# Query-key products of eight attention maps: three passes over 64 rows, or two passes of 128 and 64 rows

## The chip, the cores and the metric

The kernel runs on one core of a Trainium2 chip. The metric is the device time of one execution in microseconds, lower is better. The core has a matrix engine (TensorE, PE in the profile, with its weight loads as PEld), three engines for elementwise work (VectorE is DVE, ScalarE is ACT, GpSimd is POOL) and SyncE (SP), which issues most of the transfers. Each engine works through its own instructions in order and waits on semaphores.

## The reference, cut to what matters

The reference computes two transformer blocks over a sequence of 512 positions with model width 1024, in float32. The change lies in the second block's attention, which has 16 query-key products of head dimension 64:

```python
# stick-breaking attention, 8 heads (S in the kernel)
z = einsum('bhqd,bhkd->bhqk', q, k) * scale          # d = 64, S = 512
...
# differential attention, 4 heads of 2 maps (D in the kernel)
logits = einsum('bhqd,bhkd->bhqk', q, k) * scale + bias
probs = softmax(where(causal, logits, -inf))
w = probs[:, :, 0] - lam * probs[:, :, 1]
out = einsum('bhqk,bhkd->bhqd', w, v)
```

Both are causal, so of the 4 x 4 blocks of 128 x 128 only the lower triangle is computed: four matmuls of 128, 256, 384 and 512 columns for a map.

## The kernel before, in words

Every matrix product is made from float32 values that are split in a high part (rounded to the matrix engine's fp32r format) and a low part, the rest. A product is three matmuls ("passes") into the same accumulator: high x high, high x low and low x high. The helper `mm3` (L1723) issues them, through `mm` (L1720), so that nearly all matmuls have line L1721.

The order of the work is a plan, a list of small steps that `make_plan` (L121) writes out by hand. Each engine walks through the same list and does its own part of each step; semaphore waits are counted from the plan. Weights come in 312 units of 128 x 1024 values. SyncE loads unit u+3 when unit u has been split (L773 to L776); ACT makes the high part `wh`, DVE the low part `wl`.

In the attention stage (units 204 to 227) the plan mixes two kinds of matrix work. One is the projection: "single" steps, each three passes of 128 rows x 512 columns with a weight tile, and "vg" steps with 256 columns. The other is the heads. The pieces of the heads stand in the table `ATT_AT` (L60): a key `(224, 5)` says behind which eighth of which unit they come, and `D5.0` is step 0 of the differential pair n=5.

After the two units of a pair n are done, the step `aqev` (L1014 for ACT, L1442 for DVE) writes four tiles into a slot of `aq`: high and low of the query part (index 0 and 1) and high and low of the key part (2 and 3), each [128, 512]. Rows 0 to 63 belong to one head or map and rows 64 to 127 to the other. `aq` has three slots, used in turn. The query-key products read 64 rows of it:

- S steps 0 (L2030 to L2043) compute head b of an even n, keys stationary, columns 384, 128, 256, 512 in this order, each with `mm3`: 12 matmuls.
- D steps 0 and 3 (L2080 to L2093) compute map m = 0 or 1 of an odd n, queries stationary, columns 512, 128, 256, 384: 12 matmuls.
- The heads of n=0 are computed together by step S2 (L2006).

```python
for i in (3, 0, 1, 2):
    w = 128 * (i + 1)
    t = mm3(ps[:, ROFF[i]:ROFF[i] + w], q[pp, 0, 128 * i:128 * i + 128],
            q[pp, 1, 128 * i:128 * i + 128], q[pp, 2, 0:w], q[pp, 3, 0:w], True, True)
```

`pp` is rows 0 to 63 or 64 to 127. The order of pairs in the plan is n = 0, 1, 2, 3, 4, 5, 7, 6. D5.0, the first map of pair 5, comes behind (224, 5); the last `aqev` of pair 5 comes behind (223, 7), with the short steps `S41.0` in between in the plan of unit 223.

During the attention stage the residual x is saved to memory by POOL (step `upx`, L1677, semaphore `s_spill`), and the memory of x takes the attention outputs, one 512-column slice after another. Slices 2, 3, 5, 6 and 7 are written only by later heads. `R1`, `ssq` and `ssg` are not read in the later part of the stage.

Of the kernel before, what the change touches and what calls it, by code (L numbers as in the profile page):

```python
# [7 lines left out]
F32 = mybir.dt.float32  # L8
F32R = mybir.dt.float32r
# [373 lines left out]
def _build(nc, D, out, ctx):  # L383
    plan = make_plan()

    def sem(name):
        return ctx.enter_context(nc.semaphore(name))

    def sb(name, shape, dt=F32, stack=None):
        return (stack or ctx).enter_context(nc.sbuf_tensor(name, shape, dt))  # L390
# [9 lines left out]
    eps5 = sb("eps5", [128, 1])  # L400
    rcs = sb("rcs", [128, 4, 4])
    sb("pad", [128, 88])
    x = sb("x", [128, 8, 512])
    xh = sb("xh", [128, 8, 512], F32R)
    xl = sb("xl", [128, 8, 512], F32R)
    wraw = sb("wraw", [128, 3, 1024])
    wh = sb("wh", [128, 3, 1024], F32R)
    wl = sb("wl", [128, 3, 1024], F32R)
    R = sb("R", [128, 512])
    R1 = sb("R1", [128, 512])  # L410
    ssq = sb("ssq", [128, 512])
    ssg = sb("ssg", [128, 512])
    ones = sb("ones", [128, 128])
    onesr = sb("onesr", [128, 128], F32R)
    ident = sb("ident", [128, 128])
# [163 lines left out]

    def sig(name, **emits):
        return Sig(sem(name), plan, **emits)

# [23 lines left out]
    s_tb = sem("s_tb")  # L608
    s_misc, s_bif, s_spill, s_mg, s_p = (sem(n) for n in ("s_misc", "s_bif", "s_spill", "s_mg", "s_p"))
    s_mgb = [sem(f"s_mgb{j}") for j in range(8)]  # L610
    s_back = [sem(f"s_back{i}") for i in range(2)]
    s_b8 = [sem(f"s_b8{i}") for i in range(2)]
    s_out = [sem(f"s_out{j}") for j in range(8)]
# [146 lines left out]
    @block.sync  # L760
    def _(e):
        def load(u):
            e.dma_start(wraw[:, u % 3, :], units[u]).then_inc(s_w[u % 3], 16)

        for kind, *a in plan:
            if kind == "init":
                for j in range(8):
                    e.dma_start(x[:, j, :], D["xT"][:, j, :]).then_inc(s_x[j], 16)
                    if j == 1:
                        part(e, 3)  # L770
                    if j == 3:
                        load(2)
            elif (kind == "split" or (kind == "split0" and a[0] >= 2)) and \  # L773
                    (u := a[0] if kind == "split" else a[0] - 2) + 3 < NU:
                e.wait_ge(*wl_done(u))
                load(u + 3)  # L776
            elif kind == "last":
                for n, j in enumerate(END_ORDER):
                    if n % 2:
                        e.wait_ge(*(end_g if j in (2, 5) else end_d).at("x", j))  # L780
                        e.dma_start(out[:, j, :], x[:, j, :]).then_inc(s_out[j], 16)
                for j in END_ORDER:
                    e.wait_ge(s_out[j], 16)
# [935 lines left out]
    def _(e):  # L1719
# [3 lines left out]
        def mm3(dst, ah, al, bh, bl, start, stop, skip=False):  # L1723
            mm(dst, ah, bh, start, False, skip)
            mm(dst, ah, bl, False, False, skip)
            return mm(dst, al, bh, False, stop, skip)
# [19 lines left out]
        for kind, *a in plan:  # L1746
# [276 lines left out]
            elif kind == "S":  # L2023
# [6 lines left out]
                if s == 0:  # L2030
                    e.wait_ge(*aq_d.at(n, 1))
                    if head_before["S", n, b]:
                        e.wait_ge(*head_free(head_before["S", n, b]))
                    elif c == 1:
                        e.wait_ge(*av_d.at(0, 0, 3))
                    else:
                        e.wait_ge(*nm_a.at("R1"))
                    for i in (1, 3, 2, 0):
                        t = mm3(ps[:, OFF[i]:OFF[i] + 512 - 128 * i], q[pp, 2, 128 * i:128 * i + 128],
                                q[pp, 3, 128 * i:128 * i + 128], q[pp, 0, 128 * i:512], q[pp, 1, 128 * i:512],  # L2040
                                i != 3, True, skip=True)
                        if i in (2, 0):
                            t.then_inc(S_p.sem, 1)  # L2043
                elif s == 5:
                    if (n, b) == (6, 0):
                        unread(bank(2), 8)
                    for half, group in enumerate(((1, 3, 2), (0,))):
                        e.wait_ge(*S_d.at(n, b, f"l{half}"))
                        if (n, b, half) == (0, 1, 0):
                            e.wait_ge(*att_g.at("tri"))  # L2050
                        for i in group:
                            dst = ps[:, OFF[i]:OFF[i] + 512 - 128 * i]
                            r = slice(OFF[i], OFF[i] + 512 - 128 * i)
                            mm(dst, tri[:, :], hh[:, r], False, False, True)
                            t = mm(dst, tri[:, :], ll[:, r], False, i == 3, True)
                            for j in range(i + 1, 4):
                                w = slice(OFF[j], OFF[j] + 512 - 128 * j)
                                dj = dst[:, 128 * (j - i):]
                                mm(dj, onesn[:, :], hh[:, w], False, False, True)
                                t = mm(dj, onesn[:, :], ll[:, w], False, j == 3, True)  # L2060
                        t.then_inc(S_p.sem, 1)
                elif s == 9:
                    o = ps[:, 0:512]
                    if (n, b) == (6, 0):
                        unread(bank(2), 7)
                    for j in (1, 2, 3, 0):
                        e.wait_ge(*S_d.at(n, b, "x1" if j == 0 else "x0"))
                        e.wait_ge(*av_d.at(0, n // 4, j))
                        r = slice(OFF[j], OFF[j] + 512 - 128 * j)
                        w = slice(64 * (n - n % 2), 64 * (n - n % 2) + 128)  # L2070
                        t = mm3(o[:, 128 * j:512], av[:, j, 0, w], avl[:, j, 0, w], hh[:, r], ll[:, r], j == 1, j == 0,
                                skip=True)
                    t.then_inc(S_p.sem, 1)
            elif kind == "D":
# [5 lines left out]
                if s in (0, 3):  # L2080
                    m = 0 if s == 0 else 1
                    pp = slice(64 * m, 64 * m + 64)
                    if m == 0:
                        e.wait_ge(*aq_d.at(n, 1))
                        e.wait_ge(*head_free(head_before["D", n]))
                    else:
                        e.wait_ge(*D_d.at(n, "r02"))
                    for i in (3, 0, 1, 2):
                        w = 128 * (i + 1)
                        t = mm3(ps[:, ROFF[i]:ROFF[i] + w], q[pp, 0, 128 * i:128 * i + 128],  # L2090
                                q[pp, 1, 128 * i:128 * i + 128], q[pp, 2, 0:w], q[pp, 3, 0:w], True, True)
                        if i in (3, 2):
                            t.then_inc(D_p.sem, 1)  # L2093
                elif s == 7:
                    if n == 7:
                        e.wait_ge(*D_d.at(n, "r12"))
                    for j in range(4):
                        for i in range(3, j - 1, -1):
                            if n == 7 and j == 0 and i >= 2:
                                unread(bank(1), 7)  # L2100
                            if j == 0 and i >= 2:
                                e.wait_ge(*D_d.at(n, "w3" if i == 3 else "w2"))
                            t = e.transpose(ps[:, OFF[j] + 128 * (i - j):OFF[j] + 128 * (i - j) + 128],  # L2103
                                            pm0[:, ROFF[i] + 128 * j:ROFF[i] + 128 * j + 128], ident[:, :])
                        if j in (0, 3):
                            t.then_inc(D_p.sem, 1)
                elif s == 10:
                    o = ps[:, 0:512]
                    w = slice(128 * h, 128 * h + 128)
                    for j in range(4):  # L2110
                        if j < 2:
                            e.wait_ge(*D_d.at(n, f"l{j}"))
                        e.wait_ge(*av_d.at(1, h // 2, j))
                        r = slice(OFF[j], OFF[j] + 512 - 128 * j)
                        t = mm3(o[:, 128 * j:512], av[:, j, 1, w], avl[:, j, 1, w], hh[:, r], ll[:, r], j == 0, j == 3)
                    t.then_inc(D_p.sem, 1)
                elif s == 12:
                    if n == 7:
                        unread(bank(1), 4)
                    e.wait_ge(*D_a.at(n, "sq"))  # L2120
                    col_sums(ps[:, 512:1024], pm0).then_inc(D_p.sem, 1)
                elif s == 15:
                    e.wait_ge(*D_d.at(n, "dg"))
                    mm(ps[:, 512:1024], ones[:, :], pm0[:, 0:512]).then_inc(D_p.sem, 1)
# [171 lines left out]
```

## Time and profile before

| what | value |
|---|---|
| median of 3 runs | 1918.7 us (1918.05 to 1920.92) |
| the profiled execution's own time | 1917.96 us |
| its span, first to last instruction | 1916.1 us |
| mean granted TensorE clock | 0.996 |
| instructions in the span | 21280 |
| PE matmuls | 8718 |

The span is a little shorter than the execution's time, which also holds what lies ahead of the first and behind the last profiled instruction (1.86 us). A row of the timeline gives the start in us, the length in us, the engine, the line, the operation, the tiles as out<-in, the form (rows x stationary columns, rows x moving columns) and how many equal instructions were merged. The length of one matmul includes its way through the array; matmuls overlap, so what one costs in a stream is the distance between its start and the next start.

### The profile page before, as it was taken

Reading aid. Unit: us, or ns where it says so; the run is one execution under the profiler, and the core shown is the slowest. Engines: PE = TensorE matmul, PEld = TensorE weight load, DVE = VectorE, ACT = ScalarE, POOL = GpSimd, SP = SyncE. Lnnn points to the kernel's source line nnn. Section 1 sums busy time; section 2 is a strip of 40 time slices with the busy share of each in tenths; the row PEclk is TensorE's granted clock in tenths of the full one; section 3 lists DMA queues with packets and bytes.
Section 4 is the critical chain, followed back from the end, with each engine's and each line's share of the span. In section 5 each row is a group of like instructions: output and inputs, shape, how many; then the busy total and the mean of one; then the engine's idle time right before and its main releaser. Section 6 shows DMA issues by size and latency. Waiting matters only on the chain.

```text
span 1916.1 us, 21280 instructions
## 1 busy us (share of the span) xinstructions
PE 1892.6 (99%) x8718; PEld 1559.7 (81%) x8718; DVE 1019.6 (53%) x1283; ACT 794.5 (41%) x1060; POOL 227.7 (12%) x257
## 2 busy tenths in 40 slices
PE   9999999999999999999999999999999999999997
PEld 7888888878888788888888888888878888888885
DVE  4444443347354666664344444655565777774335
ACT  5423222236444566442232222555564444443234
POOL 2000001201300111130000022100004100000212
PEclk9999999999999999999999999999999999999998
DMA  4432322342241322423323223322113323233231
GB/s 159 157 108 88 99 99 98 103 149 93 77 138 61 98 88 87 144 88 99 99 89 109 91 96 100 121 67 67 67 44 110 100 88 109 89 98 104 96 110 55
DMA packets 51937, 188.98 MB, mean 99 GB/s; under 512 B 6568, under 2 KB 6824, under 8 KB 50944
## 3 DMA queue, kind: packets, MB, share of 16 engines
q1 hardware_dynamic: 46512, 166.09, 26.1%
q0 software_dynamic: 4176, 19.82, 3.0%
q8 instruction: 69, 1.13, 0.2%
q10 hardware_dynamic: 1152, 1.71, 0.2%
q14 instruction: 28, 0.23, 0.0%
HBM read 179.18 MB, written 11.03 MB: 99 GB/s over the span
## 4 chain that ended last, share of the span: by engine, by line
PE 95%; DVE 2%; ACT 2%; issue 1%; DMA 0%; DVEq 0%; ACTq 0%
PE psum L1721 95%; ACT at L798 1%; DMA wraw<-in_w_ffn 0%; PE psum L2103 0%; DVE x L1130 0%; ACT wh L798 0%; DVE wl L1136 0%; DVE at L1485 0%; DVE sl L1136 0%; ACT L794 0%; DVE bst L1231 0%; DVE az L1133 0%; ACT tm L798 0%; DVEq L379 0%; DVE al L1136 0%
## 5 line engine op out<-in xcount | busy, mean ns | idle before, releaser
L1721 PE MATMUL psum<-xh,wh 128*128 128x512 f32 x1760 | 694.6, 395 | 3.0 <-DVE xl L1133 2.7
L1721 PE MATMUL psum<-xh,wl 128*128 128x512 f32 x1760 | 685.8, 390 | 0.0
L1721 PE MATMUL psum<-xl,wh 128*128 128x512 f32 x1760 | 685.8, 390 | 0.0
L1136 DVE TENSOR_TENSOR wl<-wraw,wh 128x1024 fp32r<-128x1024 f32 (+1 forms) x314 | 401.1, 1285 | 402.7 <-ACT wh L798 401.7
L798 ACT ACTIVATE wh<-wraw 128x1024 fp32r<-128x1024 f32 (+1 forms) x314 | 325.6, 1047 | 367.6 <-PE psum L1721 363.9
L1721 PEld LDWEIGHTS psum<-xh,wh 128*128 128x128 f32 x1760 | 330.8, 188 | 80.5 <-issue 12.0
L1721 PEld LDWEIGHTS psum<-xl,wh 128*128 128x128 f32 x1760 | 330.9, 188 | 69.8 <-issue 2.9
L1721 PEld LDWEIGHTS psum<-xh,wl 128*128 128x128 f32 x1760 | 330.8, 188 | 69.3
L1583 POOL TENSOR_TENSOR ssq<-x 128x512 f32<-128x512 f32 x5 | 5.2, 1040 | 714.4 <-DVE x L1215 454.1
L1721 PE MATMUL psum<-wh,xh 128*128 128x512 f32 (+1 forms) x256 | 88.3, 345 | 0.4 <-ACT zv L798 0.4
L1721 PE MATMUL psum<-wh,xl 128*128 128x512 f32 (+1 forms) x256 | 86.0, 336 | 0.0
L1721 PE MATMUL psum<-wl,xh 128*128 128x512 f32 (+1 forms) x256 | 86.0, 336 | 0.0
L1721 PE MATMUL psum<-hha,wh 128*128 128x512 f32 x176 | 68.5, 389 | 0.0
L1721 PE MATMUL psum<-hla,wh 128*128 128x512 f32 x176 | 68.5, 389 | 0.0
L1721 PE MATMUL psum<-hha,wl 128*128 128x512 f32 x176 | 68.5, 389 | 0.0
L1721 PE MATMUL psum<-hhb,wh 128*128 128x512 f32 x176 | 68.5, 389 | 0.0
L1721 PE MATMUL psum<-hlb,wh 128*128 128x512 f32 x176 | 68.5, 389 | 0.0
L1721 PE MATMUL psum<-hhb,wl 128*128 128x512 f32 x176 | 68.5, 389 | 0.0
L1721 PE MATMUL psum<-hhc,wh 128*128 128x512 f32 x176 | 68.5, 389 | 0.0
L1721 PE MATMUL psum<-hlc,wh 128*128 128x512 f32 x176 | 68.5, 389 | 0.0
L1721 PE MATMUL psum<-hhc,wl 128*128 128x512 f32 x176 | 68.5, 389 | 0.0
L1133 DVE SCALAR_TENSOR_TENSOR ftc<-ftc,cols 128x511 f32<-128x511 f32 x88 | 64.1, 749 | 7.9 <-ACT ftc L798 6.4
(303 smaller groups left out, 2210.1 us busy)
## 6 DMA issues: line engine op xcount, KB each, us to landing
wraw<-in_w_ffn SPq DMA_DIRECT2D x86, 512.0 KB, 3.2
wraw<-in_w_down SPq DMA_DIRECT2D x44, 512.0 KB, 3.2
wraw<-in_w_up SPq DMA_DIRECT2D x44, 512.0 KB, 3.4
wraw<-in_w_qg SPq DMA_DIRECT2D x28, 512.0 KB, 3.3
wraw<-in_w_att SPq DMA_DIRECT2D x24, 512.0 KB, 3.3
wraw<-in_w_dn SPq DMA_DIRECT2D x22, 512.0 KB, 3.3
wraw<-in_w_zu SPq DMA_DIRECT2D x16, 512.0 KB, 3.3
wraw<-in_w_zv SPq DMA_DIRECT2D x8, 512.0 KB, 3.4
```

The lines of the kernel that those rows point to most:

```text
L798: return e.activation(dst, src, func, **kw)
L1133: return e.scalar_tensor_tensor(out=dst, in0=p, scalar=s, in1=q, op0=op0, op1=op1)
L1136: return e.tensor_tensor(dst, src, hi.bitcast(F32), ALU.subtract)
L1583: e.tensor_tensor(ssq[:, :], x[:, j, :], x[:, j, :], ALU.mult).then_inc(sq.sem, 1)
L1721: return e.matmul(dst, lhsT, rhs, start=start, stop=stop, skip_group_check=skip)
```

## The change

The stack buffers lie in the memory of x (`xr`) and of `R1`, `ssq`, `ssg` (`rr`). No memory is added. For n = 1, 3, 5 (both maps) and for head b=1 of n = 2, 4, which is eight maps, SyncE makes two new tiles by transfers within on-chip memory, once `aqev` of the pair is done:

- `st`: the high part of the stationary operand in the map's own 64 rows and its low part in the other 64 rows
- `mv`: the high part of the moving operand, in both halves

A matmul over all 128 rows with `st` and `mv` gives high x high plus low x high in one pass. The third product, high x low, stays a matmul over the map's own 64 rows. There are four transfers of 64 rows x 2 KB (128 KB) for a map, 32 in all. PE waits for them (`s_st`, 4 x 16) ahead of each map. The pieces of n = 0, 6, 7 and head b=0 of n = 2, 4 stay as they are.

```diff
+    STACK = {1: (xr[:, 2, :], xr[:, 3, :], xr[:, 6, :], xr[:, 7, :]), 2: (None, None, xr[:, 6, :], xr[:, 7, :]),
+             3: (xr[:, 5, :], rr[:, 0, :], rr[:, 1, :], rr[:, 2, :]), 4: (None, None, xr[:, 6, :], xr[:, 7, :]),
+             5: (xr[:, 6, :], rr[:, 0, :], rr[:, 1, :], rr[:, 2, :])}
...
+    s_st = {(n, b): sem(f"s_st{n}{b}") for n in STACK for b in range(2) if n % 2 or b}
... # SyncE
+        def copy(dst, src):
+            return e.dma_start(dst.bitcast(F32), src.bitcast(F32))
...
+            elif kind == "aqev" and a[0] in STACK and a[1] == 1:
+                n = a[0]
+                q = aq[:, slot_of[n], :, :]
+                (sh_, sl_), mh = ((q[:, 0, :], q[:, 1, :]), q[:, 2, :]) if n % 2 else ((q[:, 2, :], q[:, 3, :]), q[:, 0, :])
+                up, dn = slice(0, 64), slice(64, 128)
+                e.wait_ge(*aq_d.at(n, 1))
+                e.wait_ge(s_spill, 32)
+                if n == 2:
+                    e.wait_ge(*D_p.at(1, "q12"))
+                elif n == 4:
+                    e.wait_ge(*S_p.at(2, 1, "q0"))
+                elif n == 5:
+                    e.wait_ge(*D_p.at(3, "q12"))
+                    e.wait_ge(*S_p.at(4, 1, "q0"))
+                for b in range(2):
+                    st, mv = STACK[n][2 * b:2 * b + 2]
+                    own, other = (up, dn) if b == 0 else (dn, up)
+                    if st is not None:
+                        copy(st[own, :], sh_[own, :]).then_inc(s_st[n, b], 16)
+                        copy(st[other, :], sl_[own, :]).then_inc(s_st[n, b], 16)
+                        copy(mv[own, :], mh[own, :]).then_inc(s_st[n, b], 16)
+                        copy(mv[other, :], mh[own, :]).then_inc(s_st[n, b], 16)
... # PE, S step 0 (b == 1 of n = 2, 4)
+                    if n in STACK and b == 1:
+                        st, mv = STACK[n][2:]
+                        e.wait_ge(s_st[n, 1], 64)
...
+                            mm(d, st[:, 128 * i:128 * i + 128], mv[:, 128 * i:512], i != 3, False, True)
+                            t = mm(d, q[pp, 2, 128 * i:128 * i + 128], q[pp, 1, 128 * i:512], False, True, True)
... # PE, D steps 0 and 3
+                    if n in STACK:
+                        st, mv = STACK[n][2 * m:2 * m + 2]
+                        e.wait_ge(s_st[n, m], 64)
...
+                            mm(d, st[:, 128 * i:128 * i + 128], mv[:, 0:w], True, False)
+                            t = mm(d, q[pp, 0, 128 * i:128 * i + 128], q[pp, 3, 0:w], False, True)
```

## Rows read from the trace of the kernel before

**Rows 1.** The page: busy time by engine, and the chain that ended last by engine

```profile
PE 1892.6 (99%) x8718; PEld 1559.7 (81%) x8718; DVE 1019.6 (53%) x1283; ACT 794.5 (41%) x1060; POOL 227.7 (12%) x257
...
PE 95%; DVE 2%; ACT 2%; issue 1%; DMA 0%; DVEq 0%; ACTq 0%
```

**Rows 2.** Waits of PE from 1200 to 1480 us: total, times, longest (us)

```profile
PE psum L1721 <- ACT az L798: 1.7, 1, 1.7
PE psum L2103 <- DVE az L1133: 1.5, 2, 1.1
```

**Rows 3.** Timeline of PE around head S21 (n=2, b=1): start, length, line, tiles, form, count

```profile
1296.34 0.28 PE L1721 MATMUL psum<-wh,xl 128*128 128x256 f32 x1
1296.55 2.17 PE L1721 MATMUL psum<-aq 64*128 64x384 f32 x12
1298.65 0.45 PE L1721 MATMUL psum<-ah,tri 128*128 128x384 f32 x1
1298.94 0.34 PE L1721 MATMUL psum<-al,tri 128*128 128x384 f32 x1
1299.12 0.28 PE L1721 MATMUL psum<-ah,onesn 128*128 128x256 f32 x1
```

**Rows 4.** Timeline of PE inside S21: its second and its last matmul

```profile
1296.83 0.33 PE L1721 MATMUL psum<-aq 64*128 64x384 f32 x1
...
1298.33 0.39 PE L1721 MATMUL psum<-aq 64*128 64x512 f32 x1
```

**Rows 5.** Timeline of PE behind map D1.3: the next projection tile

```profile
1264.55 0.50 PE L1721 MATMUL psum<-xh,wh 128*128 128x512 f32 x1
1264.89 0.40 PE L1721 MATMUL psum<-xl,wh 128*128 128x512 f32 x1
1265.12 0.39 PE L1721 MATMUL psum<-xh,wl 128*128 128x512 f32 x1
```

**Rows 6.** Timeline of PE, 12 matmuls of 128 rows, same widths (S steps 9)

```profile
1250.47 0.28 PE L1721 MATMUL psum<-wh,xl 128*128 128x256 f32 x1
1250.60 0.34 PE L1721 MATMUL psum<-ah,av 128*128 128x384 f32 x1
...
1251.47 0.22 PE L1721 MATMUL psum<-ah,av 128*128 128x128 f32 x1
1251.53 0.28 PE L1721 MATMUL psum<-al,av 128*128 128x128 f32 x1
...
1252.49 0.28 PE L1721 MATMUL psum<-wh,xh 128*128 128x256 f32 x1
```

**Rows 7.** Timeline of all engines before D5.0: the last part of aq, D5.0, SP's next load

```profile
1369.78 0.69 DVE L1136 TENSOR_TENSOR aq<-tma,aq 128x512 fp32r<-128x512 f32 x1 [0.75 <-ACT aq L798]
...
1372.32 0.49 PE L1721 MATMUL psum<-aq 64*128 64x512 f32 x1
...
1372.47 0.33 SPq L763 DMA_DIRECT2D wraw<-in_w_ao  x1
```

**Rows 8.** Timeline for pair 1: the last part of aq, and the first matmul of D1.0

```profile
1240.42 0.69 DVE L1136 TENSOR_TENSOR aq<-tma,aq 128x512 fp32r<-128x512 f32 x1 [0.70 <-ACT aq L798]
...
1258.07 0.49 PE L1721 MATMUL psum<-aq 64*128 64x512 f32 x1
```

**Rows 9.** Timeline of SP at the start of the kernel: four transfers issued in a row

```profile
3.83 2.23 SPq L768 DMA_DIRECT2D x<-in_xT  x4
```

**Rows 10.** The page's transfers: tiles, queue, count, KB each, median us to landing

```profile
x<-in_xT SPq DMA_DIRECT2D x8, 256.0 KB, 7.8
...
b<-e8r POOLq DMA_DIRECT2D x8, 256.0 KB, 3.1
...
out_y<-x SPq DMA_DIRECT2D x4, 256.0 KB, 2.2
```

**Rows 11.** Windows: busy time of PE, PEld, DVE, ACT, POOL, then clock, DMA share, GB/s

```profile
1370.00:1380.00 10.00, 10.00 (x47) 7.72 (x46) 7.73 (x17) 4.34 (x7) 1.03 (x4) 1.00 0.15 52
1426.00:1427.50 1.50, 1.38 (x10) 1.33 (x11) 0.26 (x2) 1.31 (x3) 0.18 (x1) 1.00 0.00 0
```

More of the change, by code:

```diff
@@ L402, in _build @@
     sb("pad", [128, 88])
-    x = sb("x", [128, 8, 512])
+    xs_ = ExitStack()
+    x = sb("x", [128, 8, 512], F32, xs_)
+    xs_.close()
+    xr = sb("xr", [128, 8, 512], F32R)
     xh = sb("xh", [128, 8, 512], F32R)
@@ L409, in _build @@
     R = sb("R", [128, 512])
-    R1 = sb("R1", [128, 512])
-    ssq = sb("ssq", [128, 512])
-    ssg = sb("ssg", [128, 512])
+    rs_ = ExitStack()
+    R1 = sb("R1", [128, 512], F32, rs_)
+    ssq = sb("ssq", [128, 512], F32, rs_)
+    ssg = sb("ssg", [128, 512], F32, rs_)
+    rs_.close()
+    rr = sb("rr", [128, 3, 512], F32R)
     ones = sb("ones", [128, 128])
@@ L2037, in _ @@
                         e.wait_ge(*nm_a.at("R1"))
+                    if n in STACK and b == 1:
+                        st, mv = STACK[n][2:]
+                        e.wait_ge(s_st[n, 1], 64)
                     for i in (1, 3, 2, 0):
-                        t = mm3(ps[:, OFF[i]:OFF[i] + 512 - 128 * i], q[pp, 2, 128 * i:128 * i + 128],
-                                q[pp, 3, 128 * i:128 * i + 128], q[pp, 0, 128 * i:512], q[pp, 1, 128 * i:512],
-                                i != 3, True, skip=True)
+                        if n in STACK and b == 1:
+                            d = ps[:, OFF[i]:OFF[i] + 512 - 128 * i]
+                            mm(d, st[:, 128 * i:128 * i + 128], mv[:, 128 * i:512], i != 3, False, True)
+                            t = mm(d, q[pp, 2, 128 * i:128 * i + 128], q[pp, 1, 128 * i:512], False, True, True)
+                        else:
+                            t = mm3(ps[:, OFF[i]:OFF[i] + 512 - 128 * i], q[pp, 2, 128 * i:128 * i + 128],
+                                    q[pp, 3, 128 * i:128 * i + 128], q[pp, 0, 128 * i:512], q[pp, 1, 128 * i:512],
+                                    i != 3, True, skip=True)
                         if i in (2, 0):
@@ L2087, in _ @@
                         e.wait_ge(*D_d.at(n, "r02"))
+                    if n in STACK:
+                        st, mv = STACK[n][2 * m:2 * m + 2]
+                        e.wait_ge(s_st[n, m], 64)
                     for i in (3, 0, 1, 2):
                         w = 128 * (i + 1)
-                        t = mm3(ps[:, ROFF[i]:ROFF[i] + w], q[pp, 0, 128 * i:128 * i + 128],
-                                q[pp, 1, 128 * i:128 * i + 128], q[pp, 2, 0:w], q[pp, 3, 0:w], True, True)
+                        if n in STACK:
+                            d = ps[:, ROFF[i]:ROFF[i] + w]
+                            mm(d, st[:, 128 * i:128 * i + 128], mv[:, 0:w], True, False)
+                            t = mm(d, q[pp, 0, 128 * i:128 * i + 128], q[pp, 3, 0:w], False, True)
+                        else:
+                            t = mm3(ps[:, ROFF[i]:ROFF[i] + w], q[pp, 0, 128 * i:128 * i + 128],
+                                    q[pp, 1, 128 * i:128 * i + 128], q[pp, 2, 0:w], q[pp, 3, 0:w], True, True)
                         if i in (3, 2):
```

## The prediction, made before the changed kernel ran

> **What bounds the kernel now.** I read the page's engine totals first: PE is busy 99% of the span, DVE 53%, ACT 41% [rows 1]. The chain that ended last is PE for 95% of its length [rows 1]. So the time is PE's stream of matmuls, and an edit counts by what it does to the distance between starts on PE, or by a wait that it puts into that stream. The waits of PE come next: in the stage that is changed (1200 to 1480 us) they are 1.7 us on ACT and twice, 1.5 us together, on DVE [rows 2]; the rest of the stage runs without a pause. The other engines have room. Then the timeline of PE around a changed map, where the reader is to look at starts and not at lengths.
>
> **Part 1: eight maps, from 12 matmuls to 8.** What a matmul costs in a stream is the distance to the next start: 0.18 us for 384 columns (1298.94 to 1299.12, [rows 3]), 0.06 for 128 (1251.47 to 1251.53, [rows 6]), 0.13 for 256 (1250.47 to 1250.60, [rows 6]) and 0.23 for 512 (1264.89 to 1265.12, [rows 5]). One pass over a map's four widths is thus 0.6 us, nearer to 0.59 before the rows' rounding. If that were all, four matmuls less in eight maps would give back 8 x 0.59 = 4.7 us.
>
> But a map does not cost three times 0.59. Between the tile of 128 rows ahead of S21 and its first matmul of 64 rows lie 0.21 us (1296.34 to 1296.55) instead of 0.12 [rows 3], and that first matmul, 384 columns wide, holds the second off for 0.28 (1296.55 to 1296.83) instead of 0.18 [rows 3, 4]: 0.09 + 0.10. Going back to 128 rows, the last matmul of 64 rows (512 columns) takes 0.32 to the next start (1298.33 to 1298.65) instead of 0.23, and the one after it 0.29 instead of 0.18 [rows 3, 4]: 0.09 + 0.11. So each change between 64 and 128 rows costs 0.20 us. It is not a semaphore: the tile behind D1.3 continues a unit, waits for nothing, and shows the same 0.34 instead of 0.23 [rows 5]. Nor is it the change from projection to head: the 12 matmuls at 1250.60 have the widths of S21 and a wait ahead of them, but 128 rows, and start 0.13 us after the one before; they take 1.89 us to the next start [rows 6], which is 3 x 0.59 and 0.12 for loads that the short ones do not cover.
>
> Now a map costs 0.09 + 2.10 + 0.11 = 2.30 us [rows 3], with two changes of row count. After the edit each of its four blocks is one matmul of 128 rows and then one of 64, between streams of 128 rows: eight changes. That gives 2 x 0.59 + 8 x 0.20 = 2.78 us, 0.48 more than now, and 8 x 0.48 = 3.8 us for the eight maps. The bounds: the 0.12 us of uncovered loads of [rows 6] may come on top (2.90 us, 4.8 in all), and a change may cost less when it is made again at once; the end on that side is no cost inside the map at all (a rival below). I take 0.20 for each, since each change that the rows show has it, in both directions and behind 256 and 512 columns.
>
> The Trainium skill says in "TensorEngine Tiling (Array Packing)", section Tiling Modes (Key Properties), that changing the tiling mode, and not just the tile, drains TensorE. It names no price. The trace agrees by the 0.20 us above, and it is a rule that speaks against this change; without it the sum would be that of the second rival, and with it the 3.8 us stand.
>
> **Part 2: the wait for the transfers, pair by pair.** Pair 1 has its last part of aq at 1240.42 + 0.69 = 1241.1 and starts D1.0 at 1258.07 [rows 8]: 17 us for transfers, which hides them. Pairs 2, 3 and 4 are placed as far or farther apart in the plan (S21 at 1296.55 [rows 3] comes three units behind its aqev). Pair 5 is not: its last part is ready at 1369.78 + 0.69 = 1370.5, and D5.0 starts at 1372.32 [rows 7], 1.8 us later. In that time SP would have to issue four transfers, and all must land. SP stands free at that moment, since its next load is only issued at 1372.47 [rows 7]. Transfers in a row on SP: four in 2.23 us, so up to 0.6 apart [rows 9]; one alone occupies it 0.33 [rows 7]. I take 0.45, so the fourth goes out at 1370.5 + 3 x 0.45 = 1371.85. Landing: 2.2 us after issue for SP's out_y of 256 KB from on-chip memory, 3.1 for POOL's b [rows 10]; no row shows 128 KB within on-chip memory. I take the 2.2, the same queue and source: 1374.05, with the wait's own delay 1374.1, and PE stands for 1.8 us. Bounds: 0.33 apart and 2.2 give 1373.7 (1.4 us), 0.6 apart and 3.1 give 1375.4 (3.1 us). D5.3 stands a whole unit later in the plan (at least 8 x 3 x 0.23 = 5.5 us) and finds its four landed. PE has nothing else in this time, because its stream is in order: all projection tiles behind D5.0 stand with it.
>
> **Part 3: SP's queue.** Behind the waits of SP stand the weight loads. They are issued three units ahead; the longest delay is the eight issues of pairs 1, 3 and 5, 8 x 0.45 = 3.6 us, against 5.5 us of projection alone for a unit, and no wait of PE or ACT on a weight transfer is in the list [rows 2]. Cost 0; if the cover were gone it would be those 3.6 us. The waits on the spill and on older maps in SP's new step name work that is done earlier in the plan. The 4 MB of copies meet DMA engines that are busy 15% [rows 11]. Cost 0. The clock stays: in the pause of 1.7 us at 1426 it is granted at 1.00 [rows 11].
>
> **Part 4: what PE waits for later.** The two waits on DVE, the larger 1.1 us, end chains that start from the map's last matmul; both that start and PE's arrival move together, so they stay. The same goes for the 1.7 us on ACT, which belongs to a head that is not changed [rows 2]. At most a few tenths come back. I take 0.
>
> **Sum.** 3.8 + 1.8 = 5.6 us on the profiled execution's 1917.96 us: 1923.6. The median shown is 0.7 above that execution, so the time to compare is 1918.7 + 5.6 = 1924.3 us.
>
> **Rivals.** Forecast (a): each change of row count costs 0.20 us, and D5.0 waits. 0.74.
>
> (b) Faster: the 0.20 us belong to entering and leaving the run over aq, not to each change; inside a map a 64-row matmul follows a 128-row one as in a stream. Then a map costs 2 x 0.59 + 2 x 0.20 + 0.08 = 1.66 us, 0.64 less, 5.1 in all, and with the stall of 1.8 the time is 1915.4. For it: no row shows one matmul of 64 rows between two of 128. Against it: the cost appears on both sides, without a wait, and not in a run of 128 rows with other operands [rows 5, 6]. It decides from a price c inside a map at which 2 x 0.59 + 8 x c falls below 2.30 less the stall's share of 0.23: c under 0.11 us. 0.08.
>
> (c) Half: inside a map only the uncovered load (0.10) is paid, the gap ahead (0.09) is hidden. 2 x 0.59 + 8 x 0.10 = 1.98, 0.32 less, 2.6 in all, less the 1.8: 1917.9, no change that shows. The two halves of the price are seen apart in [rows 3, 4], which speaks for such a split, but each is there each time. 0.10.
>
> (d) The stall is the bound: the four copies queue and land like the first loads of x, 7.8 us after issue [rows 10]. Then they land at 1379.7, PE stands 7.3 us, and the time is 1929.8. Against it: those loads met each other at the kernel's start, here the DMA share is 0.15 [rows 11]. 0.08.
>
> **How the numbers follow.** A measurement of this kernel tells about 0.2% (3.8 us) from no change. (a) has its own range from 1922 (a little comes back, short stall) to 1926.6 (4.8 + 3.1 = 7.9 us above 1918.7). (b) lies below by 3.3 us, at the edge of what shows. The range for 8 in 10 goes from 1920.5 to 1926.8: (c) and (b) are left out below, (d) above. Slower by over 0.2%: (a) but for its low tail, and (d), 0.76. Within: (c), the tail and part of (b), 0.17. Faster: 0.07.
>
> **What would show it.** In the trace after: (1) a changed map takes some 2.7 us from its first start to the next stream, in eight matmuls, where starts behind a 64-row matmul of 512 columns stand near 0.43 us apart (0.23 + 0.20); if they are 0.23 apart, (b) holds. (2) One new wait of PE, at D5.0, of 1.4 to 3.1 us on a DMA; none at D1.0, D3.0, S21, S41. (3) 32 transfers on SP that land 2 to 3 us after issue. (4) PE's matmul count 32 lower, DVE's and ACT's unchanged. Wrong would be: a map shorter than 2.2 us, no wait at D5.0, or late weights.

## The result, and the profile after

| | before | after |
|---|---|---|
| median of 5 runs each | 1918.7 us (1917.88 to 1920.92) | 1927.1 us (1926.15 to 1928.54) |
| profiled execution, span | 1917.96 us, 1916.1 us | 1927.1 us, 1925.4 us |
| matmuls on PE | 8718 | 8686 |

The ratio is 1.0042 with a 95% interval of 1.0030 to 1.0054: slower by 0.3 to 0.5%, with 32 matmuls less. The medians stand 8.4 us apart. The measured median lies 2.8 us above the forecast and 0.3 us above the upper end of the range, which is less than the noise: the ratio times 1918.7 us is 1926.8, with 1924.5 to 1929.1 as its interval. The direction was right.

The waits of PE from 1200 to 1500 us, columns as in [rows 2]:

```profile
PE psum L1761 <- DMA rr<-aq: 2.3, 1, 2.3
PE psum L1761 <- ACT az L838: 1.7, 1, 1.7
PE psum L2159 <- DVE az L1173: 1.5, 2, 1.0
```

One wait is new, on the transfers of pair 5; those of [rows 2] are there as before. (PE also has 1.2 us of idle time ahead of step S2 that the profile puts down to no other engine, and three short waits of 0.2 or 0.3 us, in both kernels.) The timeline of PE around head S21 answers to [rows 3, 4]:

```profile
1296.43 0.28 PE L1761 MATMUL psum<-wh,xl 128*128 128x256 f32 x1
1296.56 0.34 PE L1761 MATMUL psum<-xr 128*128 128x384 f32 x1
1296.82 0.44 PE L1761 MATMUL psum<-aq 64*128 64x384 f32 x1
1297.19 0.33 PE L1761 MATMUL psum<-xr 128*128 128x128 f32 x1
1297.45 0.32 PE L1761 MATMUL psum<-aq 64*128 64x128 f32 x1
1297.70 0.38 PE L1761 MATMUL psum<-xr 128*128 128x256 f32 x1
1298.02 0.38 PE L1761 MATMUL psum<-aq 64*128 64x256 f32 x1
1298.33 0.50 PE L1761 MATMUL psum<-xr 128*128 128x512 f32 x1
1298.75 0.49 PE L1761 MATMUL psum<-aq 64*128 64x512 f32 x1
1299.17 0.44 PE L1761 MATMUL psum<-ah,tri 128*128 128x384 f32 x1
1299.45 0.33 PE L1761 MATMUL psum<-al,tri 128*128 128x384 f32 x1
```

The first matmul of 128 rows starts 0.13 us behind the tile of 256 columns, as in a stream: nothing changes there. The next start is 0.08 us later than 384 columns need (0.26 instead of 0.18), and from then on each is 0.18 to 0.20 later: 0.37 for 384 columns, 0.26 and 0.25 for 128 (instead of 0.06), 0.32 and 0.31 for 256 (instead of 0.13), 0.42 for 512 (instead of 0.23). The map takes 2.61 us to the next start and 0.10 more behind it: about 2.72, against 2.30 before. That is 0.42 us for each of eight maps, 3.4 us in all.

The timeline of PE at D5.0, and of SP ahead of it, answers to [rows 7]:

```profile
1376.48 0.47 PE L1761 MATMUL psum<-rr,xr 128*128 128x512 f32 x1 [2.32 <-DMA rr<-aq]
1376.88 0.57 PE L1761 MATMUL psum<-aq 64*128 64x512 f32 x1
...
1379.82 0.69 PE L1761 MATMUL psum<-aq 64*128 64x384 f32 x1
1380.44 0.79 PE L1761 MATMUL psum<-xh,wh 128*128 128x512 f32 x1
...
1383.59 0.58 PE L1761 MATMUL psum<-xl,wh 128*128 128x512 f32 x1
1384.01 0.39 PE L1761 MATMUL psum<-xh,wl 128*128 128x512 f32 x1
1384.24 0.40 PE L1761 MATMUL psum<-xh,wh 128*128 128x512 f32 x1
```

```profile
1372.23 1.11 SPq L781 DMA_DIRECT2D xr<-aq  x2
1373.38 3.81 SPq L781 DMA_DIRECT2D rr<-aq  x6
1377.23 0.59 SPq L778 DMA_DIRECT2D wraw<-in_w_ao  x1
```

The page's row of these transfers gives KB each and the time to landing:

```profile
xr<-aq SPq DMA_DIRECT2D x20, 128.0 KB, 2.3
rr<-aq SPq DMA_DIRECT2D x12, 128.0 KB, 2.3
```

Six copies take 3.81 us, so they go out 0.64 us apart (the first three gaps, 1372.23 to the fourth at 1374.0, are 0.60 on average); the fourth is D5.0's last and lands 2.3 us later. D5.0 would have started about 0.3 us behind the start of the matmul at 1373.78 and starts at 1376.48, so PE loses 2.5 us. And the matmuls behind the pause are long: 0.63 us for 512 columns where 0.39 is usual, until 1384. The windows (columns as in [rows 11]) say why:

```profile
1376.00:1384.00 8.00, 7.52 (x16) 4.89 (x17) 2.74 (x11) 0.00 (x0) 0.13 (x1) 0.57 0.47 129
1377.20:1383.90 6.70, 6.70 (x15) 4.50 (x15) 2.64 (x11) 0.00 (x0) 0.00 (x0) 0.50 0.41 118
```

The granted clock from 1376 to 1384 is 0.57 on average: in windows of 1 us it is 1.00 through the pause and until 0.7 us behind its end, and then 0.50 (1.2 GHz instead of 2.4) for 6.8 us, in which PE is never idle. From D5.0 to D5.3 PE needs 10.52 us instead of 7.09; less the 0.42 of the map, the clock costs 3.0 us. It falls once more behind the old pause of 1.7 us in the output projection, where before it did not [rows 11]:

```profile
1435.00:1439.00 4.00, 4.00 (x13) 3.29 (x14) 2.56 (x6) 0.98 (x3) 0.00 (x0) 0.57 0.00 0
```

There the stretch from map S60 to map S61 takes 18.75 us instead of 17.58, 1.2 us more.

The account, from the start of step S2 to the start of S61 in the timelines: 213.3 us before (1223.51 to 1436.77), 223.3 after (1222.76 to 1446.10), 10.1 more before rounding. Maps 3.4, wait before D5.0 2.5, clock behind it 3.0, clock behind the old pause 1.2: together 10.1. The span grew by 9.3, since the kernel's start, which is not touched, was 0.8 us shorter in this execution. That start scatters: S2 begins between 1222.1 and 1225.3 us in the 14 profiles of this document, so stretches inside a profile are compared more sharply than total times.

### The profile page after: what moved, and what is told of

Read it like the earlier page. It is cut to its first block, busy times and chain, and to the rows that moved or that the text cites. A ratio compares the mean times of both kernels' runs of the same rounds, so it can differ in the third digit from the quotient of the medians.

```text
span 1925.4 us, 21257 instructions
## 1 busy us (share of the span) xinstructions
PE 1900.1 (99%) x8686; PEld 1560.9 (81%) x8686; DVE 1019.2 (53%) x1283; ACT 794.6 (41%) x1060; POOL 227.6 (12%) x257
## 4 chain that ended last, share of the span: by engine, by line
PE 96%; ACT 2%; DVE 1%; issue 1%; DMA 0%; DVEq 0%; SPq 0%; ACTq 0%
PE psum L1761 95%; ACT at L838 1%; PE psum L2159 0%; DVE x L1170 0%; DMA wraw<-in_w_ffn 0%; ACT wh L838 0%; DVE at L1525 0%; DVE sl L1176 0%; ACT L834 0%; DVE wl L1176 0%; DMA rr<-aq 0%; DVE az L1173 0%; ACT tm L838 0%; DVEq L379 0%; SPq L781 0%
```

## The experiments

All are compared with the kernel before in runs on the same chip (the medians of before there: 1918.0 for E1 to E4, 1918.4 for E5 to E8, 1918.3 for E9 to E12). The theory: each change between 64 and 128 rows costs PE 0.2 us; pair 5 adds a wait; the wait adds time at half clock. The rivals put the loss on the transfers or on the stacked tiles. The mean granted clock is on record for every execution, not only for the profiled one.

**E1, pair 5 as before.**

```diff
-             5: (xr[:, 6, :], rr[:, 0, :], rr[:, 1, :], rr[:, 2, :])}
```

> Pair 5 goes back to three passes over 64 rows; pairs 1 to 4 (six maps) keep the two passes and their transfers. Theory (each change between 64 and 128 rows costs PE about 0.19 us, and the rest of the loss hangs on pair 5's wait): the six maps take 2.73 us each against 2.30, so 6 x 0.42 = 2.5 us over the kernel before; no wait of PE on a transfer, clock full in the whole stage. Rival (the loss comes from the transfers and their contention, wherever they run): 20 to 24 of 32 transfers stay, so some 5 to 6 us of the 8.4 us stay.

1922.2 us, ratio 1.0020 (1.0011 to 1.0029), 4.1 us above before. PE waits for no transfer, D5.0 to D5.3 takes 7.09 us, the clock there is 1.00, and the six maps take 2.72 us each. From S2 to S61 it is 3.7 us more than before: 2.5 in the maps, as expected, and 1.2 behind the old pause, where the clock fell here too. So the 24 transfers that stay delay nobody. The profiled execution (1919.3 us) is the fastest of the eleven, though, and its S2 began 1.4 us earlier than in the profile of before; the median was not profiled.

**E2, transfers and waits without the two passes.**

```diff
-                        if n in STACK:
-                            d = ps[:, ROFF[i]:ROFF[i] + w]
+                        if False:
+                            d = ps[:, ROFF[i]:ROFF[i] + w]
```

(and the same for S.)

> All 32 transfers and PE's waits on them stay, but PE computes all maps with the three passes over 64 rows of before (the stacked tiles are read by nobody). Theory: maps at 2.30 us as before, but PE stands about 2.5 us before D5.0, and behind this wait the clock is halved for some 7 us, 3.0 us more: 5.5 us over before. Rival A (the clock falls because of the mixed matmuls of 128 and 64 rows, not because of the wait): full clock behind D5.0, 2.5 us over before. Rival B (transfers cost nothing, all of the loss is in the maps): same as before.

1923.6 us, ratio 1.0027 (1.0017 to 1.0038), 5.5 us above before. All maps take 2.30 us. The timeline of PE at D5.0:

```profile
1375.36 2.15 PE L1761 MATMUL psum<-aq 64*128 64x512 f32 x12 [2.37 <-DMA rr<-aq]
1377.44 0.50 PE L1761 MATMUL psum<-xh,wh 128*128 128x512 f32 x1
```

The wait is there (2.4 us), and the clock falls behind it in a kernel without any stacked matmul: D5.0 to D5.3 takes 8.68 us, 1.6 more than before. So rival A falls: the mixed matmuls are not needed for it. In this profile the loss was 1.6 us (3.4 us at half clock) and not 3.0, and another 1.1 came behind the old pause. So the median meets the forecast of 5.5 us, but not by its terms, and that is luck. The eight times form two groups: four from 1921.3 to 1922.7 us with a mean clock of 0.995 or 0.996, and four from 1924.4 to 1925.3 us with 0.993 or 0.994. The profile is of the first group. One and the same kernel thus loses different amounts of clock from execution to execution, and about 3 us with it.

**E3, the wait filled.**

```diff
+                        if (n, m) == (5, 0):
+                            unread(bank(3), 10)
                         e.wait_ge(s_st[n, m], 64)
```

> The changed kernel with ten extra matmuls of 128 x 512 (their result is overwritten) ahead of the wait before D5.0, so that PE works for about 2.2 us of the 2.5 us in which it stood. Theory (the pause lets the clock fall): the maps and the wait keep their price, the clock stays at 1.00 behind D5.0, and the time is 3.0 us below the changed kernel, about 5.5 us over before. Rival (the clock falls for another reason, the mixed matmuls or the transfers): no gain, 8.4 us over before.

1925.7 us, ratio 1.0037 (1.0025 to 1.0050), against 1.0042 and 1.0050 of the changed kernel. In the profile the clock behind D5.0 is 1.00 and D5.0 to D5.3 takes 7.63 us instead of 10.52: the loss of 3.0 us is gone in this execution, as this window shows.

```profile
1378.00:1386.00 8.00, 8.00 (x31) 5.53 (x30) 4.58 (x13) 2.67 (x4) 0.00 (x0) 1.00 0.44 123
```

From S2 to S61 it takes 220.3 us instead of 223.3. But the median stands 7.6 us above before, where the changed kernel stands 8.4 and 9.4 above it in its two series, and the intervals overlap. (S2 began 1.8 us later than in the profile of the changed kernel, which hides part of the gain in the profiled execution.) One profile can't show that the fill is what held the clock; E11 has the same fill and comes out otherwise.

**E4, the third product over all 128 rows** (it adds the other map's product, so it is not the same sum).

```diff
-                            t = mm(d, q[pp, 0, 128 * i:128 * i + 128], q[pp, 3, 0:w], False, True)
+                            t = mm(d, q[:, 0, 128 * i:128 * i + 128], q[:, 3, 0:w], False, True)
```

(S likewise.)

> The changed kernel, but the third product of the eight maps reads all 128 rows of the pair's tiles instead of the map's own 64, so it also adds the other map's product: the same number of matmuls, the same columns, no change of row count inside a map. Theory (the price is the change of row count): a map falls from 2.73 us to 1.2 to 1.3 us, 8 x 1.45 = 11.6 us less than the changed kernel; wait and clock behind it as they are: 3 us below before. Rival (the price comes with the stacked tiles, or with alternating between tiles): maps stay near 2.7 us and the time 8.4 us over before.

1914.9 us, ratio 0.9983 (0.9974 to 0.9992). The same eight matmuls with the same columns take 1.27 us, at S21:

```profile
1295.97 0.34 PE L1761 MATMUL psum<-xr 128*128 128x384 f32 x1
1296.14 0.34 PE L1761 MATMUL psum<-aq 128*128 128x384 f32 x1
1296.32 0.22 PE L1761 MATMUL psum<-xr 128*128 128x128 f32 x1
...
1297.24 0.34 PE L1761 MATMUL psum<-ah,tri 128*128 128x384 f32 x1
```

Only the row count of every second matmul differs from the changed kernel. (2.72 - 1.27) / 8 = 0.18 us for a change. The theory stands, the rival falls: stacked tiles, alternation between tiles and two matmuls in a row into the same accumulator are all still there. PE's waits on DVE rose from 1.5 to 2.3 us, so a little of a faster map is given back. That the total meets the forecast of 3 us below before is partly luck: D5.0's wait (2.8 us) is there, but no clock was lost behind it, which the forecast had at 3 us.

**E5, the same matmuls in another order**: four of 128 rows, then four of 64.

```diff
+                    if n in STACK:
+                        for i in (3, 0, 1, 2):
+                            w = 128 * (i + 1)
+                            mm(ps[:, ROFF[i]:ROFF[i] + w], st[:, 128 * i:128 * i + 128], mv[:, 0:w], i != 2, False, True)
```

(then the second products in a loop of their own; S likewise.)

> The changed kernel, but a map issues its four matmuls of 128 rows first and then its four of 64 rows: the same eight matmuls, two changes of row count instead of eight. Theory (0.19 us for each change): a map falls from 2.73 us to about 1.6 (six changes less, 6 x 0.19 = 1.1), 8 x 1.1 = 9 us below the changed kernel; the wait before D5.0 (2.5 us) and the slow clock behind it (up to 3 us) stay: within 1 us of before. Rival (any pair of passes over the stacked tiles costs this much, the order is indifferent): maps stay at 2.7 us, 8 us over before.

1919.1 us, ratio 1.0002 (0.9993 to 1.0011). The timeline at S21:

```profile
1297.16 0.80 PE L1761 MATMUL psum<-xr 128*128 128x384 f32 x4
1297.89 0.90 PE L1761 MATMUL psum<-aq 64*128 64x384 f32 x4
1298.72 0.44 PE L1761 MATMUL psum<-ah,tri 128*128 128x384 f32 x1
```

1.56 us and 0.10 behind it, with two changes, for what takes 2.72 with eight. The order alone takes back 1.06 us a map, 8.5 in all, with D5.0's wait (2.8 us) still there. The rest of the total moved too: in this profile the clock costs 1.6 us behind D5.0 instead of 3.0 and nothing behind the old pause (S60 to S61 in 17.57 us), and the waits on DVE rose from 1.5 to 2.5 us.

**E6, E5 without D5.0** (28 transfers; `5: (None, None, rr[:, 1, :], rr[:, 2, :])`).

> As the regrouped kernel, and map D5.0 goes back to three passes over 64 rows (its tiles can't be there in time), so seven maps and 28 transfers are left. Theory: each of the seven maps takes about 1.6 us against 2.30 before, 7 x 0.65 = 4.5 us less; no wait of PE on a transfer and full clock behind D5.0: 4 to 5 us below before, 1913.5. Rival (transfers hold PE up also where it does not wait): at before or slower.

1914.5 us, ratio 0.9982 (0.9973 to 0.9990): 3.8 us below before, that is 4.5 from the maps less 1.0 in longer waits on DVE (2.5 us, as in E5), near enough. No wait on a transfer. Its profile caught an execution (1917.4 us) that lost 2.8 us behind the old pause (S60 to S61 in 20.34 us); eight of the eleven times lie between 1913.9 and 1915.5 us, three between 1916.7 and 1918.0.

**E7, two full passes, no change of row count** (seven maps; buffers and SP's waits on them are moved to make room for the third tile).

```diff
-                        copy(mv[own, :], mh[own, :]).then_inc(s_st[n, b], 16)
-                        copy(mv[other, :], mh[own, :]).then_inc(s_st[n, b], 16)
+                        for half in (own, other):
+                            copy(mv[half, :], q[own, m0_, :]).then_inc(s_st[n, b], 16)
+                            copy(ml[half, :], q[own, m0_ + 1, :]).then_inc(s_st[n, b], 16)
...
-                            t = mm(d, q[pp, 0, 128 * i:128 * i + 128], q[pp, 3, 0:w], False, True)
+                            t = mm(d, st[:, 128 * i:128 * i + 128], ml[:, 0:w], False, True)
```

> Seven maps (not D5.0) with two passes of 128 rows each and the same stationary tile, high part over low part: first against the high part of the moving operand in both halves, then against its low part in both halves (so low x low is added, which the reference has too). No change of row count at all, six transfers for a map instead of four. Theory: a map takes 1.27 us, as the run with all products over 128 rows showed, against 2.30: 7 x 1.03 = 7.2 us below before, 1911. Rival (42 transfers on SP, 0.64 us apart, delay the weight loads): PE waits on weights behind pairs 1 and 3, and part of the 7.2 us is lost.

1911.2 us, ratio 0.9963 (0.9950 to 0.9977): 7.1 us below before, and the fastest of all. The maps take 1.27 us, no transfer and no weight is waited for. PE's waits in the stage:

```profile
PE psum L2162 <- DVE az L1175: 2.3, 2, 1.4
PE psum L1763 <- ACT az L840: 1.7, 1, 1.7
```

The waits on DVE are 0.8 us longer than in [rows 2]: the chain of D1 and D3 that ends there does not get faster with PE.

**E8, the kernel before again.**

> The kernel before, unchanged, for a second profile. In all profiles since (the changed kernel and four experiments) the clock is halved for some 4 us behind the pause of 1.7 us in the output projection (1426 us in the profile of before), and the stretch from S60 to S61 takes 18.7 us instead of 17.6. Theory (this happens by execution, whatever the kernel): S60 to S61 may take 18.7 us here too, and single times scatter by over 1 us. Rival (the change brings it): 17.6 us here again.

1918.6 us, ratio 1.0000. S60 to S61 takes 17.57 us again, the clock is 1.00. This speaks for the rival as far as it was put.

**E9, the changed kernel again.**

> The changed kernel, unchanged, for a second profile. Of four kernels with a pause of 2.3 to 2.8 us at D5.0, three showed the clock halved behind it for 3 to 8 us of work (1.5 to 3 us lost), one not at all; behind the pause of 1.7 us in the output projection it was halved in five of ten profiles. Theory (whether the clock falls behind such a pause changes from execution to execution): the loss behind D5.0 here is another one than 3.0 us, between 0 and 3, and the single times scatter by more than those of before. Rival (it belongs to the kernel): 3.0 us behind D5.0 and 1.2 us behind the other pause again.

1927.7 us, ratio 1.0050 (1.0038 to 1.0063). The second profile gives the first one's numbers: wait 2.3 us, D5.0 to D5.3 10.52 us, S60 to S61 18.76. So my theory that it is a matter of the execution got no support from this profile. But both profiles are of executions with the lowest mean clock of their five, 0.993; the others have up to 0.996. Over all ten, those with 0.995 or 0.996 take 1926.7 us on average and those with 0.993 or 0.994 take 1928.2. (The clock had been halved behind the old pause in six of the ten profiles, not five: E6 belongs to them.)

**E10, the kernel before with its old pause filled** (`unread(bank(1), 11)` instead of 4 ahead of D7.12).

> The kernel before with 11 instead of 4 extra matmuls ahead of step D7.12, which fills its pause of 1.7 us. Theory (the pause costs clock in some executions only): S60 to S61 takes 17.6 us as in the two profiles of before, and the median falls by a few tenths, at most 1.2 us. Rival (the pause never costs clock in the kernel before): no difference.

1918.3 us, ratio 0.9997 (0.9988 to 1.0006). The pause is gone from the list of waits, S60 to S61 takes 17.57, the time is the same. In its profiles the kernel before loses no clock there that could be won back.

**E11, the changed kernel with both pauses filled.**

> The changed kernel with both pauses filled (ten extra matmuls ahead of D5.0's wait, 11 instead of 4 ahead of D7.12). Theory: full clock in the whole stage, and what is left over the kernel before is the maps (8 x 0.42 = 3.4 us) and the wait (2.5 us): 5.9 us, against 8.4 us of the changed kernel. Rival (the clock is not the missing part): 8 us over before as without the fill.

1923.4 us, ratio 1.0027 (1.0017 to 1.0036), 5.1 us above before and 4.3 us below the changed kernel (E9) on the same chip. The mean clock of its ten executions is 0.996 to 0.998, against 0.993 to 0.995 in E9: with both fills less clock is lost, and the time is less. The 5.1 us also lie near the 5.9 of the maps and the wait, but the profiled execution, which has the median's time, does not divide that way. From S2 to S61 it takes 7.6 us more than before (3.4 in the maps, 2.5 in the filled wait, 1.6 at half clock), and its S2 began 1.2 us earlier. The fill did not hold the clock there:

```profile
1376.00:1378.00 2.00, 2.00 (x7) 1.10 (x6) 0.85 (x3) 0.00 (x0) 0.00 (x0) 1.00 0.88 206
1378.00:1380.00 2.00, 2.00 (x7) 1.39 (x7) 1.12 (x6) 0.00 (x0) 0.00 (x0) 0.77 0.84 267
1380.00:1382.00 2.00, 2.00 (x6) 1.61 (x5) 0.71 (x2) 0.00 (x0) 0.00 (x0) 0.50 0.00 0
```

PE was busy all the time, with extra matmuls and then the mixed ones of D5.0, and still lost some 1.6 us at half clock (D5.0 to D5.3 in 9.28 us, 7.63 in E3). Up to D7.12, well behind this place, E3 and E11 are the same kernel line for line, and one execution kept the clock where the other lost it. So whether it falls at D5.0 does change from execution to execution, as E9's theory had it, and a pause of PE is not needed for it.

**E12, E7 with the old pause filled.**

> The seven maps with two full passes of 128 rows, and the pause ahead of D7.12 filled. Theory: 7.2 us below before from the maps and a few tenths more from executions in which the clock fell behind the pause: 7 to 8 us below before. Rival (the fill delays PE, since the chain it waits for ends sooner than the fill): 1 us less gained.

1912.6 us, ratio 0.9965 (0.9953 to 0.9978), against 0.9963 in E7; the times are 1909.6 twice and 1912.6 to 1913.1 three times. From S2 to S61 both profiles take 206.8 us, so no cost and no gain of the fill shows.

## Why the prediction came out as it did

**Bound.** PE's stream bounds the stage: right. Every edit that took time out of the stream came out in the total, but for 0.8 to 1.0 us in waits on DVE. The sentence that the rest of the stage runs without a pause was too strong: the profile of before has another 1.2 us of idle time ahead of S2 and three waits of 0.2 or 0.3 us. None of them changed.

**Part 1.** Right in mechanism and near in size: 0.48 us a map forecast, 0.42 measured, 3.4 instead of 3.8 us in all. A change costs 0.18 us (E4) and not 0.20. E5 shows that it is the number of changes, E4 that it is the row count. The Trainium skill says in "TensorEngine Tiling (Array Packing)", section Tiling Modes (Key Properties), that changing the tiling mode drains TensorE. The trace agrees in that each change costs 0.18 us; no row shows the drain itself. Rival (b) fell with the first look at S21, and so did (c): a change costs 0.18 to 0.20 us there, not 0.10.

**Part 2.** Right in place: the one new wait is at D5.0. The term was too small, 2.5 us instead of 1.8. SP issued the four copies over 1.8 us where I took 1.35 (0.60 apart on average, not 0.45; the upper bound in [rows 9] was the right one), which is 0.45 of the 0.7 us. The landing (2.3 against 2.2 us) and PE's start 0.2 us behind it make most of the rest. Rival (d), a landing after 7.8 us, fell. E2 shows this wait without the two passes.

**Part 3, transfers and weights.** Right: no wait on weights, and E1 has 24 transfers at no cost. The margin was thinner than forecast, since eight issues hold SP for 5.0 us (1372.23 to 1377.23) and not 3.6, against the 5.5 us of a unit.

**"The clock stays."** This step failed. I read it off one row, the pause of 1.7 us behind which the clock was 1.00 [rows 11], and carried it to a pause that is longer and in other surroundings. Behind D5.0 the clock was at half for 6.8 us and cost 3.0 us, more than the wait that preceded it; that and the 1.2 us behind the old pause are nearly all that lifted the profiled execution beyond the 5.6 us of the sum. E2 shows the fall without stacked matmuls.

What decides it is open. At D5.0 the clock fell in four of the five profiles with a pause of 2.3 to 2.8 us (not in E4), in one of the two in which the pause was filled (E11, not E3), and in none of the seven in which D5.0 waits for no transfer. That ties the fall to the wait or to what comes with it, such as the copies. That the pause itself is the cause was argued and is not shown. Where it fell it cost 3.0 us (the changed kernel, twice) or 1.6 us (E2, E5, E11). Behind the same 1.7 us pause the kernel before, E5 and E7 lost nothing, the changed kernel and E1 to E4 1.1 to 1.2 us, E6 2.8. Executions of one kernel differ in it: E2's times fall in two groups by their mean clock, and E3 and E11 are the same kernel up to this place.

**The sum.** Two errors nearly cancel: the maps cost 0.4 us less than forecast and the wait 0.7 more, so that these two terms give 5.9 us and not 5.6. The clock, put at nothing, is what the forecast lacks. That the measured median still stands at the upper end of the range is luck: the range reached up to there with a dearer map (4.8 us) and a longer wait (3.1 us), and neither came. The profile divides the 10.1 us of its own execution; how the 8.4 us between the medians divide is not shown as exactly.

**Part 4.** Right for this change; the waits on DVE stayed at 1.5 us.

## What to carry to other kernels

Count changes of row count, not matmuls: a matmul over 64 rows between matmuls over 128 costs two changes, here 0.18 us each, and a pass saved by stacking costs more than it saves if every second matmul stays at 64 rows. Keep all passes at one row count (E7), or put those of one kind together (E5). When a transfer is to be ready for an in-order engine, count its issues at the measured distance on that queue, and reckon with half clock around a pause of the matrix engine: here it cost from nothing to 3.0 us, changed from execution to execution, and filling the pause did not rule it out.

## What the runs showed of the hardware that I had not expected

- Copies of 64 rows x 2 KB within on-chip memory leave SP 0.60 to 0.64 us apart; SP is occupied for 0.33 us by a weight load that is issued alone. A copy lands after 2.3 us (median).
- Behind a pause of 2.3 us PE ran at 1.2 GHz for 6.8 us of uninterrupted work. In E11 it ran at 1.2 GHz for 3.4 us without a pause before, where E3, the same kernel up to there, stayed at 2.4 GHz.
- Two passes that are all at 128 rows cost little more than their columns: eight matmuls in 1.27 us (2 x 0.59 = 1.18 for the columns), whether the second pass has the stationary tile of the first (E7) or another (E4). The 12 over 64 rows took 2.30.
